# Cached key tiles from unit 0 on, four in one run, and query tables cleared in three parts

## The reference

```
sc = einsum('bthd,btjhd->bhtj', q, kg) * HEAD_DIM**-0.5 - slopes * (j * dil)
p  = exp(sc - logsumexp(sc));  o = einsum('bhtj,btjhd->bthd', p, vg)
```

## Time and profile before

| | us |
|---|---|
| median of the runs | 1918.85 |
| profiled execution | 1915.48 |
| its span, first to last instruction | 1913.6 |
| TensorE (PE) busy | 1877.8 (98%) |
| VectorE (DVE) busy | 638.8 (33%) |
| ScalarE (ACT) busy | 460.9 (24%) |
| GpSimd (POOL) busy | 193.3 (10%) |

### The profile page before, as it was taken

How to read it: one execution, slowest core, us unless ns; L and a number is a source line. 1 busy time by engine, 2 the same in 40 slices (tenths; PEclk the granted TensorE clock), 3 DMA queues, 4 the chain that set the end, 5 groups by cost and what they waited for, 6 DMA issues and landing times.

```text
span 1913.6 us, 44783 instructions
## 1 busy us (share of the span) xinstructions
PE 1877.8 (98%) x20479; PEld 1282.5 (67%) x20480; DVE 638.8 (33%) x1081; ACT 460.9 (24%) x688; POOL 193.3 (10%) x260
## 2 busy tenths in 40 slices
PE   8999999999999999999999999999999999999998
PEld 8998877999999998877874353534435353443535
DVE  5456543654434556643541010110201011020101
ACT  5434442444424444443431000000000000000000
POOL 2114100233403113200100000000000000000000
PEclk9999999999999999999999999999999999999999
DMA  9443799655545443689547999999999999999996
GB/s 300 144 154 123 234 310 358 202 160 159 172 158 185 152 144 130 211 287 356 187 160 265 415 383 409 404 383 409 373 415 386 404 407 382 410 375 415 385 405 267
DMA packets 212399, 553.82 MB, mean 289 GB/s; under 512 B 11482, under 2 KB 107914, under 8 KB 195680
## 3 DMA queue, kind: packets, MB, share of 16 engines
q1 hardware_dynamic: 208864, 541.71, 76.7%
q0 software_dynamic: 3248, 9.18, 1.4%
q10 hardware_dynamic: 96, 0.02, 0.0%
HBM read 543.46 MB, written 7.77 MB: 288 GB/s over the span
## 4 chain that ended last, share of the span: by engine, by line
PE 95%; DVE 2%; DMA 1%; ACT 1%; issue 1%; SPq 0%; DVEq 0%; POOL 0%; ACTq 0%; POOLq 0%
PE psum L952 89%; PE psum L960 6%; DMA low_part<-in_w_branch_attn 1%; DVE w_split L1823 1%; ACT w_split L1544 0%; DMA low_part<-in_x_sample 0%; DVE low_part L2322 0%; DVE low_part L1816 0%; DVE low_part L1935 0%; DVE high_part L1940 0%; ACT low_part L1514 0%; DVE high_part L1860 0%; DVE xn_split L1835 0%; SPq L814 0%; DVE xn_tok L2186 0%
## 5 line engine op out<-in xcount | busy, mean ns | idle before, releaser
L952 PE MATMUL psum<-low_part 128*32 128x512 f32 (+3 forms) x6926 | 675.2, 526 | 6.8 <-ACT low_part L1514 4.8
L952 PEld LDWEIGHTS psum<-xn_split,w_split 128*128 128x128 f32 x3744 | 502.8, 188 | 36.7 <-issue 31.0
L952 PE MATMUL psum<-xn_split,w_split 128*128 128x288 f32 x3744 | 519.4, 297 | 1.5 <-DVE w_split L1823 1.3
L952 PEld LDWEIGHTS psum<-low_part 128*32 128x32 f32 (+2 forms) x6926 | 239.9, 114 | 398.0 <-issue 390.1
L952 PE MATMUL psum<-low_part,high_part 128*32 128x256 f32 (+3 forms) x6636 | 343.3, 359 | 3.4 <-DVE low_part L1816 2.3
L1823 DVE TENSOR_TENSOR w_split<-low_part,w_split 128x2048 fp32r<-128x2048 f32 x104 | 238.7, 2296 | 267.0 <-ACT w_split L1544 266.8
L952 PEld LDWEIGHTS psum<-low_part,high_part 128*32 128x32 f32 (+1 forms) x6636 | 217.0, 111 | 129.2 <-issue 14.9
L1544 ACT ACTIVATE w_split<-low_part 128x2048 fp32r<-128x2048 f32 x104 | 199.1, 1914 | 264.8 <-PE psum L952 216.7
L2334 DVE TENSOR_TENSOR low_part<-high_part,psum 128x384 f32<-128x384 f32 (+1 forms) x48 | 29.8, 621 | 426.2 <-PE psum L952 423.8
L1787 ACT ACTIVATE high_part<-psum 128x384 f32<-128x384 f32 (+1 forms) x48 | 25.9, 544 | 395.0 <-PE psum L952 394.1
L960 PE MATMUL psum<-high_part,low_part 128*128 128x128 f32 (+2 forms) x839 | 109.8, 281 | 10.1 <-DMA low_part<-in_x_sample 6.9
(11 more groups left out here) (159 smaller groups left out, 942.7 us busy)
## 6 DMA issues: line engine op xcount, KB each, us to landing
low_part<-in_we_down SPq DMA_DIRECT2D x112, 1024.0 KB, 8.5
low_part<-in_cache_kv_g SPq DMA_DIRECT2D x72, 1024.0 KB, 5.7
low_part<-in_we_gate SPq DMA_DIRECT2D x64, 1024.0 KB, 8.2
low_part<-in_we_up SPq DMA_DIRECT2D x64, 1024.0 KB, 8.6
low_part<-in_w_in SPq DMA_DIRECT2D x55, 1024.0 KB, 5.1
low_part<-in_we_gate SPq DMA_DIRECT2D x64, 768.0 KB, 7.7
low_part<-in_we_up SPq DMA_DIRECT2D x64, 768.0 KB, 7.3
low_part<-in_w_dense SPq DMA_DIRECT2D x33, 1024.0 KB, 5.4
```

The costliest lines, as they stand in the source:

```text
L952: signal(e.matmul(out, lhsT, rhs, start=start, stop=stop, skip_group_check=mixed), inc)
```

## The change

Three things. Every unit from `v` = 0 to 8 now takes a whole chunk of four tiles in one run between its scores and its values, so all 36 tiles of half 0 lie in the units (`REST` = 36); `score_new` and the first chunk's scores come with tile 8, the second chunk's with tile 9. The copies on ScalarE and VectorE go by the same function, so all of a unit's copies come at head 0 (`he` = 0). The clear of the query tables is cut in three: two parts go among the row stores of step 32, the third stays.

```
-FIRST_STEP = 2
+FIRST_STEP = 0
+FIRST_SCORE = 8
 def step_tiles(v, part):
-    at = BH * (v - FIRST_STEP) + 2 * part
-    return [m for m in (at, at + 1) if 0 <= m < NT]
-REST = step_tiles(NU, 1)[-1] + 1
+    at = BH * (v - FIRST_STEP)
+    return [m for m in range(at, at + BH) if part == 0 and 0 <= m < NT]
+REST = step_tiles(NU, 0)[-1] + 1
...
-        zeroed = Tally(sem("sample_tiles_zeroed"), 4)
+        zeroed = Tally(sem("sample_tiles_zeroed"), 6)
...
                 def cache_step(m):
-                    if m in (LAG, NT + LAG + BH - 1):
+                    if m in (FIRST_SCORE, NT + LAG + BH - 1):
                         score_new(m // NT)
-                    if m >= LAG and (m - LAG) % BH == BH - 1:
+                    if m == FIRST_SCORE:
+                        score_chunk(0)
+                    elif m > FIRST_SCORE and (m - LAG) % BH == BH - 1:
                         score_chunk((m - LAG) // BH)
...
+                    if n == 32:
+                        e.wait_ge(mean_ready.sem, mean_ready.at(L, 2 * PG))
+                        e.memset(view(strips_at, work_at - strips_at), 0.0).then_inc(zeroed.sem, 1)
+                        S.wait_read(e, ("vt", 1, 2))
+                        S.wait_read(e, ("bc", 23))
+                        e.memset(view(work_at + 4 * T, strips_at + 12 * ROWS + 2 * J * BH * DS * 32 - work_at - 4 * T), 0.0)\
+                            .then_inc(zeroed.sem, 1)
                 S.wait_read(e, ("vt", 2, 2))
-                e.memset(view(strips_at, 12 * ROWS + 2 * J * BH * DS * 32), 0.0).then_inc(zeroed.sem, 1)
+                e.memset(view(work_at, 4 * T), 0.0).then_inc(zeroed.sem, 1)
...
-                e.wait_ge(zeroed.sem, zeroed.at(L, 1))
+                e.wait_ge(zeroed.sem, zeroed.at(L, 3))
```

More of the change, by code:

```diff
@@ L1704, in place_probs @@
                 S.wait_full(e, job)
-                e.wait_ge(zeroed.sem, zeroed.at(L, 4))
+                e.wait_ge(zeroed.sem, zeroed.at(L, 6))
                 ps = S.ps(job)
```

## The result

| | before | after |
|---|---|---|
| median of 9 runs each, us | 1918.85 (1916.99 to 1921.84) | 1926.75 (1922.48 to 1930.96) |
| ratio after / before | | 1.004 [1.003, 1.0051] |
| profiled execution, its own time, us | 1915.48 | 1930.82 |
| its span, us | 1913.6 | 1929.0 |
| its mean granted clock | 0.996 | 0.991 |

The change costs 7.9 us. The forecast was +4.4 us, 1923.3, so slower was right; the time lies 0.25 us above the upper end of the range, 1926.5.

What follows compares the result with a forecast made beforehand. TensorE, busy 98% of the span, bounds the kernel, so only its waits count. Terms 0.86 + 0.6 + 0.74 = 2.2 us a layer, 4.4 for two, gave 1923.3 us; range 1918.5 to 1926.5.

Steps and rivals of the forecast that it cites:

- the old one: Unit 1, before the change: values(0) waits 2.38 us for a ScalarE PSUM copy; forecast to be gone.
- tile 6: Third tile of unit 1: TensorE waits 2.77 us for its bank, until ScalarE has copied tile 4.
- The sum of waits in units 0 and 1: Waits at tiles 2, 3 and 6: 3.64 us against 2.78 before, 0.86 us worse in each layer.
- Tile 30: Unit 7, with no scores left to cover the copy of tile 28: a wait of 0.74 us, bounds 0 and 1.1.
- Clear and transfers: GpSimd's clear in three parts and earlier cache-chunk loads: each worth 0 us.
- order and waits: The whole forecast loss: 0.86 + 0.6 + 0.74 = 2.2 us a layer, 4.4 for two.
- The clock: Rival: longer gap, then score_new, bring clock drops of 1.6 us each; 1924.9 us with one more, 1926.5 with two; chance 0.10.
- units 3 to 6: Four units with four-tile runs: 0.15 us lost in each, 0.6 us a layer, possible 0 to 1.4.
- a loop: Units 3 to 6: a chain through VectorE and ScalarE takes 6.42 us against TensorE's 6.06.
- TensorE's work is the same, only moved: Tiles from unit 0 on, four in one run: no added TensorE work, only new waits for banks and copies.
- the 0.88 for turn_probs: turn_probs ahead of scores, taken from two tiles with turn_probs at 1.90 us and two tiles turned at 1.02.
- the placing of queries: GpSimd, ahead of score_new at tile 8: follows the last clear, which ends 3.83 us earlier, so no wait.

Runs made afterwards that it cites:

- the clear alone: The kernel before with only the query-table clear cut in three parts as in the change: 1920.03 us, ratio 1.0005.
- the gap filled: The changed kernel with 21 throwaway transposes ahead of tile 6, so TensorE works through the wait: 1922.78 us, ratio 1.0015.
- one clear: The changed kernel with the query tables cleared by one memset again, as before: 1927.18 us, ratio 1.0044.
- score_new in one piece: After with two-and-two tiles, unit 0's second pair behind turn_probs(0), second-half queries placed before clears: 1922.09 us; with clears held for both engines' placing: 1914.42 us.
- after with spread short matmuls: The changed kernel with score_new's three head groups at every fourth tile, nothing else: 1924.59 us, ratio 1.0023.
- score_new spread: The two-and-two version, unit 0's second pair behind turn_probs(0), with score_new's head groups every fourth tile: 1916.22 us; with GpSimd's clears held until placing is done: 1911.63 us.
- The one line that orders the two: Added to the two-and-two versions: GpSimd's probability-table clears wait until both engines placed the second half's queries; 1916.22 to 1911.63 us spread, 1922.09 to 1914.42 whole.

## Why the prediction was half right

**Right: direction, place and mechanism.** The wait that takes the place of the old one is at tile 6, for the copy of tile 4, which stands behind the scalings of unit 1: forecast 2.77, measured 2.75. The sum of waits in units 0 and 1 was put at 3.64 and is 0.29 + 0.25 + 2.75 = 3.29. Tile 30 was put at 0.74 and waits 0.66. Clear and transfers at 0: the clear alone is 1.0005 [0.9995, 1.0016]. The cost of order and waits, forecast 4.4 us, is 4.9 ± 0.8 at equal clock; from the stretches at full clock it is 5.7.

**Wrong: the clock had no term in the sum.** "The clock" was a rival with a chance of 0.10, on the ground that "right after the old gaps nothing dropped". That was one execution. In others the same 2.38 us gap was followed by a drop, and behind the 2.75 us gap both layers of the profile of after show one. The mean clock of after's runs is lower by 0.0015, 2.6 us that the sum put at nothing. The forecast with them is 1923.3 + 2.6 = 1925.9; with 5.7 us of order and waits in place of 4.4 it is 1927.2, against 1926.75 measured. The rival's ground, that the longer gap brings more drops, isn't borne out: 3 of 6 behind 2.75 us, 4 of 8 behind 2.38. Where the runs of after lose their clock is not shown: of the 15.4 us between the two profiles, 5.3 lie outside the edited stretches. The Trainium skill, in "TensorE: Matmul & The Clock Gate", section "What's actually happening", has the low clock as the state after idleness; the prediction weighed this rule and believed one trace more. The mean of the runs agrees with the rule, 0.9957 with the gap filled against 0.9930; single executions need not: with one clear the clock stayed at 1.00 behind 2.75 us of idleness.

**Near in size for a wrong reason, too small in the whole: units 3 to 6.** The prediction took 0.6 us a layer for "a loop" through VectorE and ScalarE. No wait appeared there at all. The units are longer, 6.23 for 6.06, by 0.7 in four units, because turned tiles and turn_probs no longer stand side by side on TensorE. "TensorE's work is the same, only moved" was the false sentence: the earlier trace rows had both prices, 1.90 for sixteen together and 1.02 for eight, and I even used the 0.88 for turn_probs where it still fitted. That 0.7 is near the 0.6 is luck; over the whole stretch the work grows by 70.05 - 68.79 = 1.26 us a layer, twice the term.

**Missed: the second score_new.** The prediction let the placing of queries follow a clear that ends earlier, and looked only at the first half. In the second half TensorE arrives 0.34 us before GpSimd is done, 0.7 in both layers; with one clear it does so in layer 1 alone.

**What stays open.** How often a gap of a given length is followed by a drop, since executions differ, and how much of after's loss of clock arises at score_new: score_new in one piece goes with 0.9924 where 1.67 us of idleness stand ahead of it and with 0.9953 where none do, but after with spread short matmuls (0.9938) is no better than after with one clear (0.9940). Why eight transposes between matmuls of another kind cost 1.02 and two sets side by side 1.90 was not taken apart.

## What to carry to other kernels

When an edit only moves work on the engine that bounds, count its seams: which neighbours of one kind it separates, with the price of a joined and a parted run from the rows. A wait of some microseconds on TensorE can cost more than its length, so an edit that leaves the wait and only moves it is not neutral; shorten it, and if that can't be done, see how the runs' clocks spread before you leave the clock out of the sum. A gain in one stage arrives only if the engines that feed the next one are earlier too: here the early tiles were worth nothing until GpSimd's placing was.

## What the runs showed of the hardware

A VectorE copy from SBUF to SBUF stood still while GpSimd cleared: 64x32 elements in 2.60 us beside two clears of 1024 elements, 0.18 undisturbed. VectorE's copies of 128x512 from PSUM kept 0.69 beside the same clears in the profile of after. The Trainium skill, in "SBUF — State Buffer", section "Who interferes with whom", says that a VectorE copy in a 2-port mode and a GpSimd instruction lock each other out of a shared port pair for a whole instruction; the trace agrees in that the copy lasts until the clears end; that these copies run in such a mode, no run shows, and the copy's record begins 0.72 us ahead of the clears. The one line that orders the two takes away two waits, 3.3 us in all: the median fell by 4.6 us with score_new spread (1916.22 to 1911.63) and by 7.7 with it in one piece (1922.09 to 1914.42); at equal clock both are 3.5.

TensorE's idleness cost beyond its length: the same 4.95 us, idle or filled, make 1926.75 or 1922.78 us, and two levels of mean clock, 0.9930 and 0.9957. It is a cost in the mean of many executions: behind a given gap the low clock came in some and not in others.
